# Later background steps in the in-projection of a decoder step, and its first key products on VectorE

## The reference, cut to what matters

```python
proj = h @ w_in                                   # the in-projection, 1024 -> 4608
rq, rk, rv, rg, dq, dk, dv = jnp.split(proj, EVEN_SPLITS, axis=-1)
ro = head_group_norm(retention(rope(rq), rope(rk), rv, s0)) * silu(rg)
dq = rope(rms_norm(dq, qg)); dk = rope(rms_norm(dk, kg))
k_all = [cache_k[page_table], dk]                 # sample rows: 8 x 32 pages of 128 keys
s = einsum(dq, k_all) * scale; p = softmax(s)
do = einsum(p[:, :, 0] - lam * p[:, :, 1], v_all) # differential attention
mix = concat([ro, rms_norm(do, sub_g) * (1 - lam_init)]) @ w_out   # the output projection
```

## Time and profile before

| | us |
|---|---|
| median of 3 runs | 2000.88 (1991.13 to 2001.93) |
| the profiled execution | 1999.38 |
| its span | 1997.5 |
| PE busy | 1868.1 (94%) |
| DVE (VectorE) busy | 905.9 (45%) |
| POOL (GpSimd) busy | 650.9 (33%) |
| ACT (ScalarE) busy | 606.0 (30%) |

### The profile page before, as it was taken

One profiled execution on the slowest core, in us unless ns is written; L12 is line 12 of the kernel. 1 busy time (PEld: TensorE's weight loads), 2 busy tenths in 40 slices (PEclk: granted clock), 3 DMA queues, 4 the chain that ended last, 5 costly groups with the idle time before them and its releaser, 6 DMA issues.

```text
span 1997.5 us, 31030 instructions
## 1 busy us (share of the span) xinstructions
PE 1868.1 (94%) x12203; PEld 1489.4 (75%) x12203; DVE 905.9 (45%) x1232; ACT 606.0 (30%) x987; POOL 650.9 (33%) x480
## 2 busy tenths in 40 slices
PE   3886998899799999999999999999999999999998
PEld 3775666666477776777769887666668799999997
DVE  3686664465658556543333226422233453223321
ACT  5432346332323231122323321132322332212311
POOL 0484343443347988444110000130121334103400
PEclk8987898899899999999999999999999999999999
DMA  7252464777777969855264665958882233323231
GB/s 252 75 182 93 152 197 159 235 253 248 260 255 259 306 230 338 273 180 184 90 194 144 190 209 185 294 188 273 259 283 88 85 95 92 96 90 91 84 104 56
DMA packets 296722, 365.43 MB, mean 183 GB/s; under 512 B 15625, under 2 KB 228186, under 8 KB 296330
## 3 DMA queue, kind: packets, MB, share of 16 engines
q1 hardware_dynamic: 289354, 355.36, 54.5%
q10 hardware_dynamic: 6640, 6.95, 1.0%
q0 software_dynamic: 592, 1.25, 0.5%
HBM read 352.29 MB, written 11.21 MB: 182 GB/s over the span
## 4 chain that ended last, share of the span: by engine, by line
PE 58%; issue 25%; DVE 7%; ACT 4%; POOL 4%; DMA 1%; SPq 1%; ACTq 0%; DVEq 0%; POOLq 0%
PE ps L2253 8%; PE ps L2255 8%; PE ps L2254 8%; PE ps L2343 6%; PE ps L2345 6%; PE ps L2344 6%; PE ps L2033 3%; PE ps L1965 2%; PE ps L1967 2%; PE ps L1966 2%; POOL tmp L950 2%; PE ps L2146 1%; DVE Sc L1562 1%; ACT w_hi L673 1%; POOL g_lo L911 1%
## 5 line engine op out<-in xcount | busy, mean ns | idle before, releaser
L680 DVE TENSOR_TENSOR w_lo<-raw,w_hi 128x1024 fp32r<-128x1024 f32 x239 | 342.2, 1436 | 458.9 <-ACT w_hi L673 458.0
L891 POOL TENSOR_TENSOR kbuf<-kbuf,Qb 128x512 f32<-128x512 f32 x256 | 372.0, 1480 | 283.4 <-DMA kbuf<-in_cache_k 283.1
L673 ACT ACTIVATE w_hi<-raw 128x1024 fp32r<-128x1024 f32 x246 | 258.4, 1055 | 476.1 <-PE ps L2255 264.8
L1965 PE MATMUL ps<-w_hi,xg_hi 128*128 128x256 f32 x576 | 189.0, 328 | 0.4 <-DVE w_lo L680 0.4
L2253 PE MATMUL ps<-xb_hi,w_hi 128*128 128x512 f32 x448 | 182.2, 407 | 0.0
L950 POOL TENSOR_TENSOR tmp<-tmp,vn 128x512 f32<-128x512 f32 x24 | 33.4, 1413 | 447.3 <-ACT tmp L1332 447.3
L2255 PE MATMUL ps<-xb_hi,w_lo 128*128 128x512 f32 x448 | 177.1, 395 | 0.0
L2254 PE MATMUL ps<-xb_lo,w_hi 128*128 128x512 f32 x448 | 176.5, 394 | 0.0
L1562 DVE TENSOR_REDUCE Sc<-kbuf 128x8 f32<-128x512 f32 x256 | 162.6, 674 | 16.8 <-POOL kbuf L891 16.7
L1966 PE MATMUL ps<-w_lo,xg_hi 128*128 128x256 f32 x576 | 169.7, 295 | 0.0
L1967 PE MATMUL ps<-w_hi,xg_lo 128*128 128x256 f32 x576 | 169.3, 294 | 0.0
(11 more groups left out here) (369 smaller groups left out, 3856.2 us busy)
## 6 DMA issues: line engine op xcount, KB each, us to landing
kbuf<-in_cache_k SPq DMA_DIRECT2D x256, 256.0 KB, 3.8
vbuf<-in_cache_v SPq DMA_DIRECT2D x256, 256.0 KB, 4.5
raw<-in_w_ffn_up SPq DMA_DIRECT2D x64, 512.0 KB, 4.1
raw<-in_w_ffn_down SPq DMA_DIRECT2D x64, 512.0 KB, 3.6
raw<-in_w_in_odd SPq DMA_DIRECT2D x48, 512.0 KB, 4.8
ring<-in_w_in_odd SPq DMA_DIRECT2D x48, 512.0 KB, 5.4
raw<-in_w_in_even SPq DMA_DIRECT2D x34, 512.0 KB, 5.0
ring<-in_w_ffn_up SPq DMA_DIRECT2D x32, 512.0 KB, 5.8
```

The lines of the kernel that those rows point to most:

```text
L673: act.activation(w_hi[:, c.slot], source(c), ACT.Copy).then_inc(hi_made, 1)
L680: dve.tensor_tensor(w_lo[:, c.slot], source(c), w_hi[:, c.slot].bitcast(F32), ALU.subtract).then_inc(lo_made, 1)
L891: pool.tensor_tensor(kk, kk, Qb[:, s % 2, :], ALU.mult).then_inc(k_weighed, 1)
L1965: pe.matmul(out, xh, wh, start=kk == 0, stop=False, skip_group_check=True)
```

## The change

*Table.* Ticks start at slot 18, not 12, and in the in-projection stand in the first and third quarter, not the second and fourth. The steps of a unit of differential attention, of a rope (now three parts), of the sample's rope (three), of the norm (`dn`, four) and of gated retention stand more quarters apart. The tail has 3 slots, not 8; of the twelve `mix` steps four stand in it and eight in the first slots of the output projection, with three banks in turn, and the output projection's chunks wait for 4, 8 and 12 mixes. In its chunks TensorE runs quarters one by one between the matmuls, no longer three at once between the blocks.

*Engines.* The products of the first `OWN_KEYS` pages of keys (those of the in-projection, 122 by the table) are VectorE's, each just ahead of its sum; GpSimd's first is the 123rd, in the tail. Every `w_lo` of the in-projection is VectorE's but for the ones made ahead of it, which do not change. `maxT` and `maxB` use the PSUM bank of `dB`, `sT` and `rB`. The write of the prompt's retention state goes from `rA` to `rB` on ScalarE, and the wait for `x_back` from ahead of the output projection to ahead of its first sum.

```diff
-FIRST_STEP = 12
-TAIL = 8
+FIRST_STEP = 18
+TAIL = 3
...
-LO_SWITCH = 4
...
-    first = 4 * (read_of(3) + 6)
+    first = 4 * (read_of(3) + 5)
     for i in range(len(UNITS)):
         at = first + 21 * i // 4
         put(("dA", i), at)
-        put(("dE", i), at + 2)
-        put(("dM", i), at + 3)
-        apart(("dT", i), "turn", at + 5)
-        apart(("dB", i), "out", at + 7)
+        put(("dE", i), at + 3)
+        put(("dM", i), at + 4)
+        apart(("dT", i), "turn", at + 8)
+        apart(("dB", i), "out", at + 10)
...
-        if m < 4:
-            put(("rope", m), at)
...
+        for part in range(3):
+            put(("rope", m, part), at + part) if m < 4 else put(("rot", m, part), at + 2 * part)
...
-        put(("dnorm", q), at + 4 * q)
-    put(("sx",), 4 * (read_of(10) + 1) + 1)
+        for part, after in enumerate((0, 1, 2, 4)):
+            put(("dn", q, part), at + 4 * q + after)
+    put(("sx",), 4 * (read_of(10) + 3) + 3)
...
-            put(("rA", h, n), at + 4 * n)
-            put(("rB", h, n), at + 4 * n + 2)
-        put(("rS", h), at + 17)
+            put(("rA", h, n), at + 4 * n + 1)
+            put(("rB", h, n), at + 4 * n + 4)
+        put(("rS", h), at + 18)
...
-        at = 4 * (read_of(10) + 6 + 6 * h)
+        at = 4 * (read_of(10) + 4 + 6 * h)
         put(("sL", h), at)
         put(("sM", h), at)
         for p in range(NS // 2):
-            put(("sU", h, p), at + 5 + 4 * p)
-        put(("sO", h), at + 21)
-    put(("so1",), 4 * (NTILE + 2) + 2)
-    put(("so2",), 4 * (NTILE + 4))
-    put(("soT",), 4 * (NTILE + 6))
-    for i in range(12):
-        put(("mix", i), 4 * NTILE + (2 * i if i < 6 else 2 * i + 2))
+            put(("sU", h, p), at + 7 + 4 * p)
+        put(("sO", h), at + 23)
+    put(("so1",), 4 * NTILE + 5)
+    put(("so2",), 4 * NTILE + 8)
+    put(("soT",), 4 * NTILE + 11)
+    for i, at in enumerate((1, 2, 3, 4, 12, 12, 13, 13, 14, 15, 16, 17)):
+        put(("mix", i), 4 * NTILE + at)
...
-            parts[j][3 if n >= due // 2 else 1].extend(ticks.pop(0))
+            if j < NTILE:
+                parts[j][2 if n == due - 1 else 0].extend(ticks.pop(0))
+            else:
+                parts[j][3 if n >= due // 2 else 1].extend(ticks.pop(0))
...
+OWN_KEYS = sum(s[0] == "K" for now in AFTER[:NTILE] for s in now)
...
+        MIXED = (4, 5, 6)
...
-                    if kind == "K":
+                for kind, i, *_ in [s + (0,) for s in AFTER[j]]:
+                    if kind == "K" and i >= OWN_KEYS:
+                        if i == OWN_KEYS:
+                            pool.wait_ge(k_weighed, i)
...
-                if 0 < m < LO_SWITCH and t == 0:
-                    lo(pool, Chunk(0, 0, 0, 2 * m + AHEAD))
...
+                    if i < OWN_KEYS:
+                        kk = kbuf[i % K_SLOTS][:, :]
+                        if g == 0:
+                            dve.wait_ge(out_read, OUT_FILL["qb", s] + 1)
+                        dve.wait_ge(k_loaded[i % K_SLOTS], 16 * (i // K_SLOTS + 1))
+                        dve.tensor_tensor(kk, kk, Qb[:, s % 2, :], ALU.mult).then_inc(k_weighed, 1)
                     dve.wait_ge(k_weighed, i + 1)
...
-                if LO_SWITCH <= m < N_IN and t == 0:
-                    if m == LO_SWITCH:
-                        dve.wait_ge(lo_made, 2 * m + AHEAD)
+                if 0 < m < N_IN and t == 0:
                     lo(dve, Chunk(0, 0, 0, 2 * m + AHEAD))
...
-                    wait(pe, outb_read, OUTB_FILL[step])
-                    turn(ps[0:NS, OUTB, 0:P], mx8, P).then_inc(outb_ready, 1)
+                    wait(pe, out_read, OUT_FILL[step])
+                    turn(ps[0:NS, OUT, 0:P], mx8, P).then_inc(out_ready, 1)
...
-                    wait(pe, mix_lo, n - 1)
+                    if n == 2:
+                        pe.wait_ge(s_placed, 1)
+                    wait(pe, mix_lo, n - 2)
...
-                            if blk == 0 and not (e is not None and m == 0 and g == 0):
-                                run(PARTS[slot_of(c.n)][:3])
+                                q = 2 * blk + k // 2
+                                if k % 2 and q < 3 and not (e is not None and m == 0 and g == 0):
+                                    run(PARTS[slot_of(c.n)][q:q + 1])
...
-            prompts("oe", mixed(ma_hi, mb_hi), mixed(ma_lo, mb_lo), mix_lo, [12, 12, 12])
+            prompts("oe", mixed(ma_hi, mb_hi), mixed(ma_lo, mb_lo), mix_lo, [4, 8, 12])
```

More of the change, by code:

```diff
@@ L162, in plan @@
         put(("dA", i), at)
-        put(("dE", i), at + 2)
-        put(("dM", i), at + 3)
-        apart(("dT", i), "turn", at + 5)
-        apart(("dB", i), "out", at + 7)
+        put(("dE", i), at + 3)
+        put(("dM", i), at + 4)
+        apart(("dT", i), "turn", at + 8)
+        apart(("dB", i), "out", at + 10)
+    for i in range(2):
+        apart(("qb", i), "out", 4 * AT[0, 2] + 4 * i)
+        for part in range(3):
+            put(("ropeS", i, part), 4 * (AT[2, 2] if i else AT[0, 0]) + 2 + part)
+    for m in range(N_IN):
+        apart(("sT", m), "out", 4 * sample_at(m) + (5 if m < 2 else 7))
+    put(("snew0",), 4 * AT[3, 0])
+    apart(("snew",), "out", 4 * AT[3, 3])
     for m in ROPED:
         at = 4 * read_of(m)
-        if m < 4:
-            put(("rope", m), at)
-        else:
-            for part in range(3):
-                put(("rot", m, part), at + 2 * part)
+        for part in range(3):
+            put(("rope", m, part), at + part) if m < 4 else put(("rot", m, part), at + 2 * part)
         for hh in range(2):
@@ L1194, in act_step @@
                                    ).then_inc(out_read, 1)
[L1195 to L1199, removed]
-                    act.activation(pq[:, 0, :], doN[:, i, :], ACT.Square).then_inc(d_sq, 1)
-                    act.wait_ge(d_ss, i + 1)
-                    act.activation(dn4, dn4, ACT.Sqrt, scale=1.0 / P, bias=EPS).then_inc(d_root, 1)
-                    act.wait_ge(d_scale, i + 1)
-                    for h in range(H):
-                        head = doN[:, i, P * h:P * h + P]
-                        last = act.activation(head, head, ACT.Copy, scale=dn4[:, h:h + 1])
-                    last.then_inc(d_done, 1)
+                elif kind == "dn":
+                    if step[2] == 0:
+                        act.wait_ge(out_read, OUT_FILL["dB", len(UNITS) - 1] + 1)
+                        act.wait_ge(turn_ready, TURN_FILL["dT", len(UNITS) - 1] + 1)
+                        wait(act, d_ss, i)
+                        act.activation(pq[:, 0, :], doN[:, i, :], ACT.Square).then_inc(d_sq, 1)
+                    elif step[2] == 2:
+                        act.wait_ge(d_ss, i + 1)
+                        act.activation(dn4, dn4, ACT.Sqrt, scale=1.0 / P, bias=EPS).then_inc(d_root, 1)
+                    elif step[2] == 3:
+                        act.wait_ge(d_scale, i + 1)
+                        for h in range(H):
+                            head = doN[:, i, P * h:P * h + P]
+                            last = act.activation(head, head, ACT.Copy, scale=dn4[:, h:h + 1])
+                        last.then_inc(d_done, 1)
                 elif kind == "sx":
@@ L1543, in dve_step @@
                 if kind == "rope":
-                    rope_step(i)
+                    rope_step(i, step[2])
                 elif kind == "rot":
@@ L1547, in dve_step @@
                 elif kind == "ropeS":
-                    rope_sample(i)
+                    rope_sample(i, step[2])
                 elif kind == "rotS":
@@ L2017, in pe_step @@
                     pe.wait_ge(row_max, i + 1)
[L2018 to L2019 removed]
+                    wait(pe, out_read, OUT_FILL[step])
+                    turn(ps[0:NS, OUT, 0:P], mx8, P).then_inc(out_ready, 1)
                 elif kind == "maxB":
                     pe.wait_ge(max_spread, i + 1)
[L2022 to L2023 removed]
+                    wait(pe, out_read, OUT_FILL[step])
+                    pe.matmul(ps[:, OUT, 0:NS], ones[0:NS, :], mxd, start=True, stop=True).then_inc(out_ready, 1)
                 elif kind == "V":
```

122 lines of the change are left out of this document (60 added, 62 removed).

## The result

The changed kernel took **1950.91 us** (median of 4 runs, 1946.51 to 1951.09) beside 2001.12 for the kernel before: a ratio of 0.9755, with a 95% interval of 0.9721 to 0.9789, or some 50 us less. The forecast was 1950. The profiled execution took 1950.76 us, its span is 1948.9.

A forecast was written before the change was run, and what follows sets the result against it. TensorE was taken to bound the kernel, losing time to waits, mostly for late VectorE, and to the slow clock they bring. Terms -8 - 26 - 10 - 11 + 4 = -51 us gave 1948, adjusted to 1950 us; range 1908 to 1990.

The forecast's parts named there:

- B: In-projection slots 18 to 45, 216 us before; forecast to fall to 190 us (-26).
- C: In-projection slots 46 to 73, 200 us before; forecast to fall to 190 us (-10).
- D: Tail from the last in-projection matmul to the first of the output projection, 31 us before; forecast -11 us.
- A: In-projection slots 2 to 17, 69 us before; forecast to fall to 61 us (-8).
- Steps 1 and 2: VectorE in the in-projection: 122 products add 41 us in B, 43 in C; lost stretch saves 8 in A, 20, 6.
- Step 5: In-projection: more quarters between steps cover most waits; half the way to the floor, A -8, B -26, C -10 us.
- Step 6: Tail: eight of twelve mixes move into the output projection, `ma_lo` waits go, 2 us left for the sample's norm; -11 us.
- Step 7: Output projection on: moved V pages add 4 us of TensorE, 18 products and sums move later, nothing else.
- Waits nearly vanish: Rival: TensorE's waits nearly vanish; A 58, B 172, C 178, D 19 us; total 1915 us; chance 0.20.
- main case: The summed forecast: -51 us, total 1950 us, with B and C at 190 us each; chance 0.50.
- VectorE full: Rival: TensorE waits for ropes and gates in VectorE's queue instead; B 205, C 196 us; total 1973 us; chance 0.15.
- Slower behind the key loads: Rival: w_lo, mixes and gates queue on VectorE behind products waiting for key pages; total 2027 us; chance 0.08.

The follow-up runs named there:

- before_da: The kernel before with only the attention unit's new spacing (exponentials 3, mix 4, transposes 8, product 10 quarters behind the scores): 1967.22 us, ratio 0.9871.
- keys_gp: The changed kernel with the in-projection's key products back on GpSimd, w_lo and table as changed: 1935.66 us, ratio 0.9713 to the kernel before.
- no_products: The changed kernel without the in-projection's key products on any engine, VectorE still waiting for and summing the pages: 1919.3 us, ratio 0.9622 to the kernel before.

## Why the prediction came out right

The total was right, the sum was not: its errors cancel, and that it came within 1 us is luck. B and C gave 20.6 us more than forecast; D gave 6.4 less, and 15.9 more was lost behind it.

| | forecast | measured |
|---|---|---|
| A | -8 | -8.4 |
| B | -26 | -40.4 |
| C | -10 | -16.2 |
| D | -11 | -4.6 |
| start of the in-projection | 0 | +1.2 |
| output projection on | +4 | +19.9 |
| sum | -51 | -48.6 |

- *What bounded it* held. Idle and clock fell together: in B idle PE by 22.4 us, time at the lower clock, worked out from the mean granted clock (0.85 and 0.90), from some 65 to 34 us.
- *Steps 1 and 2* had the durations right (0.69 against 682 ns; the stretch 20 us in B against 26.7, 6 in C against 5.8), and also that VectorE has more to do on the whole. Its need in B was put at 158 us and was 147.7. What failed is what was made of it: since VectorE was "level with PE in B and below it elsewhere", the products were let through nearly free (B to 190 us, where half of the way to the floor is 187). In the new table they cost 16.4 and 9.2 us on VectorE, and 13.7 and nothing on GpSimd with its stretch. The Trainium skill (SBUF — State Buffer, Who interferes with whom) was borne out: two-input instructions pay while GpSimd reads, sums do not (w_lo 1422 ns for 1224, sums 675 for 676). The Trainium skill (Perfetto Trace Analysis, Optimizing Scalar/DVE Operations) says that work may be taken off a saturated VectorE, even to GpSimd, but that between these two it "might not help". Here VectorE's share with the products was 0.84 in B and 0.77 in C; giving them back to GpSimd helped in C and cannot be told from nothing in B.
- *Step 5* named the right mechanism and was mis-sized. Taking "half of what lies between now and the floor" gave some -26 and -10; the table with the old engines gave -37.8 (215.5 to 177.7) and -26.3 (200.2 to 173.9). The products took part of that back in C. The forecast's cover for the mixes was right (24.5 us to 0.5).
- *Step 6* found the wait that is late next and gave it 2 us; it took 15.5. VectorE's row there was four mixes, four gates and a norm, stretched by 2.6 us beside GpSimd. The wait for `ma_lo` did go (8.7 to 1.4 us), but the clock's part did not come back (0.71 in D). As PE's work was only to move, D is to be read with the output projection, to which 32 transposes went: -4.6 and +3.7, so -0.9 for -11.
- *Step 7's* "Nothing else there" failed. The first MLP is 4.4 us longer where 4 were forecast, but PE is busy only 2.0 us longer in it (32 moved V matmuls came, 48 matmuls of the sample's later steps left); the rest is idle. So the size fits and what made it does not. Another 3.7 came in the output projection, and 11.7 in `u`: 5.8 of them idle PE, where the sample's small steps met late w_lo, the rest matmuls of the sample that came later, and the clock. That the ticks end nearer to their limit was seen; that their place beside the queues of `u` matters was not.
- *Signs.* One sign of being wrong came: a stretch behind the output projection's start longer by more than 8 us (`u`, 11.7). D was to be about 15 us and was 26.2. The first matmul of the output projection was to come at about 510 us, as if D's own -11 were not in it; the sum gives 500, and it came at 486.6. The signs of the mechanism came: `pq` waits of 0.5 us, VectorE's w_lo at 1.22, a clock of 0.90 in B.
- *Rivals.* "Waits nearly vanish" (B 172, C 178) came nearer in these two stages (175.1, 184.0) than the main case (190, 190). "VectorE full" has a part in B, as leaving the products out takes 16.4 us off it, but at 175 us, not 205. "Slower behind the key loads" did not occur: VectorE sat idle 0.1 us in all before the 60 products of B.

Open: which of the steps in C pays there, and why the products cost time in C, where VectorE is busy 0.77 of it. No run takes the shorter tail, the mixes' places, the banks or the ticks' quarters by themselves. Nor is it known how much of before_da's 27 us the rest of the change would have given without it (in the changed kernel the unit's spacing is worth 11 by the stages, 8.9 in B and 2.1 in C).

## What to carry to other kernels

Ask of each wait whether its two ends could simply stand further apart in the program before moving work between engines: four offsets gave about half of the gain here, and moving the products cost. Contention that is real in busy time need not be worth its cure; price both by leaving the work out once. And a table that moves background steps also shifts the phase of everything behind it, so look at every later stage, and add up the queue of the step that is "late next".

## What was not expected of the hardware

A step on one element for each partition (L1741) took 526 ns on the mean in B of keys_gp and 220 in no_products. Its sixteen cases in keys_gp fall into two groups: the seven that no product of GpSimd ran beside took 219 to 222 ns, the nine others 363 to 1162. A 128x1024 w_lo took 1.22 us alone and 2.25 at most there. So the small instruction lost up to 0.94 us and the large one up to 1.03: a meeting cost about as much whatever the instruction's own size, and most of GpSimd's products took some 1.3 us. That puts a price on short chains, which a sum of busy times by size does not show.
